# High and low activations joined in one product of 512 columns, loops written out, and the FFN's order of casts, drains and waits changed

## What is computed

```python
def swiglu_ffn(h, w_in, w_out):
    g, u = jnp.split(h @ w_in, 2, axis=-1)
    return (jax.nn.silu(g) * u) @ w_out
```

## Time and profile before

| | |
|---|---|
| median of 3 runs | 3946.58 us (3941.61 to 3947.43) |
| the profiled execution | 3947.24 us, its span 3945.5 us |
| mean granted clock of TensorE | 0.967 |
| TensorE busy | 3680.2 us, 93% |
| VectorE (DVE) busy | 2140.2 us, 54% |
| ScalarE (ACT) busy | 1617.5 us, 41% |
| moved by DMA | 612.34 MB, 155 GB/s |

### The profile page before, as it was taken

One profiled execution on the slowest core, in us unless ns is written; L12 is line 12 of the kernel. 1 busy time (PEld: TensorE's weight loads), 2 busy tenths in 40 slices (PEclk: granted clock), 3 DMA queues, 4 the chain that ended last, 5 costly groups with the idle time before them and its releaser, 6 DMA issues.

```text
span 3945.5 us, 60283 instructions
## 1 busy us (share of the span) xinstructions
PE 3680.2 (93%) x24695; PEld 3366.3 (85%) x24695; DVE 2140.2 (54%) x2737; ACT 1617.5 (41%) x2144; POOL 241.6 (6%) x232
## 2 busy tenths in 40 slices
PE   7888799999997999989999999999989899999998
PEld 6766799999977997768989989899777699899897
DVE  5887634555656545555444444554555554444444
ACT  4334323655643333444433333343333354333333
POOL 3562000000000020000000000000000000000000
PEclk9988899999998999989999999999998899999999
DMA  7324456555454564435656656555324356566564
GB/s 207 97 86 145 136 150 181 140 151 149 139 192 124 175 160 128 150 107 149 175 183 184 182 186 180 184 164 160 124 90 135 101 159 181 181 181 181 182 185 144
DMA packets 859333, 612.34 MB, mean 155 GB/s; under 512 B 10370, under 2 KB 752305, under 8 KB 858144
## 3 DMA queue, kind: packets, MB, share of 16 engines
q1 hardware_dynamic: 857072, 602.21, 52.3%
q0 software_dynamic: 2096, 7.81, 0.7%
HBM read 607.82 MB, written 2.16 MB: 155 GB/s over the span
## 4 chain that ended last, share of the span: by engine, by line
PE 83%; DVE 9%; ACT 3%; issue 2%; POOL 2%; DMA 0%; ACTq 0%; DVEq 0%; SPq 0%
PE acc L897 48%; PE acc L887 27%; PE psC L990 2%; DVE wL L1658 2%; PE psA L959 1%; ACT wH L1256 1%; DVE xtok L1619 1%; PE psC L945 1%; DVE arena L1965 1%; PE psB L945 1%; PE psB L973 1%; ACT L1256 1%; POOL arena L760 0%; PE psA L862 0%; DMA xtok<-in_x 0%
## 5 line engine op out<-in xcount | busy, mean ns | idle before, releaser
L1658 DVE TENSOR_TENSOR wL<-ring,wH 128x1024 fp32r<-128x1024 f32 x1128 | 1336.4, 1226 | 1125.3 <-ACT wH L1256 1120.6
L897 PE MATMUL acc<-actH,wH 128*128 128x256 f32 x5760 | 1654.8, 287 | 28.4 <-DVE wL L1658 28.4
L897 PE MATMUL acc<-actL,wH 128*128 128x256 f32 x5760 | 1632.4, 283 | 0.0
L897 PE MATMUL acc<-actH,wL 128*128 128x256 f32 x5760 | 1632.1, 283 | 0.0
L1256 ACT CAST wH<-ring 128x1024 fp32r<-128x1024 f32 x1128 | 1125.1, 1046 | 1223.2 <-PE acc L887 631.9
L897 PEld LDWEIGHTS acc<-actH,wH 128*128 128x128 f32 x5760 | 1108.3, 192 | 40.7 <-DVE wL L1658 23.0
L897 PEld LDWEIGHTS acc<-actL,wH 128*128 128x128 f32 x5760 | 1108.3, 192 | 4.8 <-issue 3.3
L897 PEld LDWEIGHTS acc<-actH,wL 128*128 128x128 f32 x5760 | 1107.7, 192 | 0.0
L887 PE MATMUL acc<-wH,actH 128*128 128x512 f32 x896 | 365.5, 408 | 25.9 <-DVE actL L1650 22.8
L887 PE MATMUL acc<-wL,actH 128*128 128x512 f32 x896 | 356.6, 398 | 0.0
L887 PE MATMUL acc<-wH,actL 128*128 128x512 f32 x896 | 355.7, 397 | 0.0
(11 more groups left out here) (294 smaller groups left out, 2488.1 us busy)
## 6 DMA issues: line engine op xcount, KB each, us to landing
ring<-in_w_ffn_in SPq DMA_DIRECT2D x176, 1024.0 KB, 5.7
ring<-in_w_ffn_out SPq DMA_DIRECT2D x88, 1024.0 KB, 5.1
ring<-in_b_w_in SPq DMA_DIRECT2D x64, 1024.0 KB, 6.2
ring<-in_w_in_ab SPq DMA_DIRECT2D x56, 1024.0 KB, 5.5
ring<-in_w_in_c SPq DMA_DIRECT2D x48, 1024.0 KB, 5.7
ring<-in_kv_w SPq DMA_DIRECT2D x24, 1024.0 KB, 5.6
ring<-in_a_w_in SPq DMA_DIRECT2D x16, 1024.0 KB, 7.1
ring<-in_w_xkv SPq DMA_DIRECT2D x16, 1024.0 KB, 5.7
```

The source lines that it names most:

```text
L897: ins = pe.matmul(dst, w[:, t, f * P:(f + 1) * P], x[:, t, :], start=t == 0 and n == 0, stop=t == ph.kt - 1 and n == 2)
L1658: dve.tensor_tensor(wL[:, split_slot, cols], ring[:, slot, cols], wH[:, split_slot, cols].bitcast(F32), ALU.subtract).then_inc(l_made, 1)
```

## The change

**The joined product.** actH and actL become the two halves of one tile act2. A feat phase that is `joined` computes per k-tile wH times both halves in one product of 512 columns, and then wL times the high half, added to the right half of the bank. The sum of left and right half is the outcome: ACT copies the left half out (`take_left`), DVE adds the right one (`add_right`). Joined are the phases named above; s5, kv_mem, b_z, ab_rg and glu stay as they were. A joined chunk takes a whole bank per feature tile, both banks of its pair.

**Loops written out.** `rep` is gone; `dense` and `stream` are Python loops on all engines. Waits for turned tiles and for splits now stand only in the first iteration.

**FFN.** Roundings of weights come ahead of drains, as in the diff; silu now reads SBUF, and a third tile `up_left` takes the left half of the up product. ffn_out waits for hidL block by block, in its first chunk.

```diff
-        actH = sb("actH", P, FT, T, dt=F32R)
-        actL = sb("actL", P, FT, T, dt=F32R)
+        act2 = sb("act2", P, FT, 2, T, dt=F32R)
+        actH, actL = act2[:, :, 0, :], act2[:, :, 1, :]
...
+        def take_left(act, ph, i, c, dst):
+            act.wait_ge(blocks_done, ph.blocks_before(i, c, ph.blocks))
+            first = 2 * ph.pair(c)
+            act.copy(dst, acc[:, first:first + 2, 0:T]).then_inc(left_out, 1)
+
+        def add_right(dve, ph, i, c, dst, left):
+            dve.wait_ge(left_out, ph.lefts(i, c))
+            first = 2 * ph.pair(c)
+            return dve.tensor_tensor(dst, left, acc[:, first:first + 2, T:2 * T], ALU.add)
...
@@ TensorE, one_block @@
-                    if c == 0 and splits:
+                    if i == 0 and c == 0 and splits:
                         pe.wait_ge(act_l, split_steps(splits[0]) + b + 1)
+                    if i == 0 and c == 0 and ph.hidden:
+                        pe.wait_ge(hid_l, hidden_before + ph.kt // 2 * (b + 1))
...
+                elif ph.joined:
+                    bank = pair[:, b, :]
+                    for t in range(ph.kt):
+                        if turn_call is not None and i == 0 and c == 0 and b == 0:
+                            pe.wait_ge(turned_l, FT * turn_call + t + 1)
+                        pe.matmul(bank.rearrange("p (h t) -> p h t", h=2), high[:, t, :], act2[:, t, :, :],
+                                  start=t == 0, stop=False)
+                        ins = pe.matmul(bank[:, T:2 * T], low[:, t, :], xH[:, t, :], start=False,
+                                        stop=t == ph.kt - 1)
...
@@ dense, on every engine @@
-                with rep(pe, ph.iters) as i:
+                for i in range(ph.iters):
...
@@ TensorE, FFN @@
-                    pe.wait_ge(hid_l, (l * FFN_T + sum(FFN_PARTS[:k + 1])) // 2)
-                    dense(ffn_out)
+                    dense(ffn_out, hidden_before=(l * FFN_T + sum(FFN_PARTS[:k])) // 2)
...
@@ ACT, one_block @@
-                if b == ph.blocks - 1 and fn is not None:
+                if b == ph.blocks - 1 and ph.joined:
+                    take_left(act, ph, i, c, feat_slot(ph, fn, i, c))
+                elif b == ph.blocks - 1 and fn is not None:
                     drain_chunk(act, ph, i, c, fn)
...
@@ ACT, FFN (cast = split_weights of block k of iteration i) @@
+                    for i in range(ffn_in.iters):
+                        cast(i, 1)
+                        if i > 0:
+                            take_left(act, ffn_in, i - 1, 1, up_left)
+                        cast(i, 2)
+                        if i > 0:
+                            hidden_high(i - 1)
+                        cast(i, 3)
+                        wait_past(act, drained[ffn_in.pair(1)], ffn_in.pair_uses(i, 1))
+                        take_left(act, ffn_in, i, 0, silu_g)
+                        act.wait_ge(drained[ffn_in.pair(0)], ffn_in.pair_uses(i, 0) + 1)
+                        act.activation(silu_g, silu_g, ACT.Silu).then_inc(silu_done, 1)
+                        cast(i, 4)
+                    take_left(act, ffn_in, ffn_in.iters - 1, 1, up_left)
+                    hidden_high(ffn_in.iters - 1)
...
@@ DVE, one_block @@
+                if b == ph.blocks - 1 and ph.joined:
+                    dst = feat_slot(ph, fn, i, c)
+                    add_right(dve, ph, i, c, dst, dst).then_inc(drained[ph.pair(c)], 1)
...
@@ DVE, FFN @@
+                    def up(i):
+                        add_right(dve, ffn_in, i, 1, hid_f, up_left).then_inc(up_summed, 1)
+                        dve.wait_ge(silu_done, i + (pairs_done + 1))
+                        dve.wait_ge(up_summed, i + (pairs_done + 1))
+                        dve.tensor_tensor(hid_f, hid_f, silu_g, ALU.mult).then_inc(drained[ffn_in.pair(1)], 1)
...
+                    for i in range(ffn_in.iters):
+                        low(i, 1)
+                        if i > 0:
+                            up(i - 1)
+                        low(i, 2)
+                        if i > 0:
+                            hidden_low(i - 1)
+                        low(i, 3)
+                        add_right(dve, ffn_in, i, 0, silu_g, silu_g).then_inc(drained[ffn_in.pair(0)], 1)
+                        low(i, 4)
+                    up(ffn_in.iters - 1)
+                    hidden_low(ffn_in.iters - 1)
```

More of the change, by code:

```diff
@@ L132, in __init__ @@
         plan["chunks"] += chunks
+        self.joined, self.joined0 = joined, plan["joined"]
+        plan["joined"] += chunks if joined else 0
         self.end = plan["chunks"]
@@ L347, in program @@
         out_done = sem("out_done")
-        plan = {"blocks": 0, "chunks": 0}
+        plan = {"blocks": 0, "chunks": 0, "joined": 0}
         def columns(w, kt, cols):
@@ L354, in columns, with feat @@
             return lambda j, k=0: v[:, k * kt:(k + 1) * kt, bass.ts(j, cols)]
-        def feat(w, first, tiles, iters=1):
+        def feat(w, first, tiles, iters=1, joined=True):
             at = columns(w, FT, P)
@@ L369, in tok @@
                          "tok", iters, hidden)
-        s5_u = feat(a["a_w_in"][0], 0, 8, 2)
-        s5_z = feat(a["a_w_in"][0], 8, 8, 2)
-        kv_mem = [(feat(a["w_xkv_2"][l], 0, XH), tok(a["w_xkv_2"][l], 1, 1, 4)) for l in range(DEPTH)]
+        s5_u = feat(a["a_w_in"][0], 0, 8, 2, joined=False)
+        s5_z = feat(a["a_w_in"][0], 8, 8, 2, joined=False)
+        kv_mem = [(feat(a["w_xkv_2"][l], 0, XH, joined=False), tok(a["w_xkv_2"][l], 1, 1, 4)) for l in range(DEPTH)]
         glu_at = columns(a["a_w_glu"][0], 8, 2 * P)
@@ L383, in program @@
             b_q.append(feat(a["b_w_in"][0], 8 * hh, 8, 2))
-            b_z.append([feat(a["b_w_in"][0], NH * (r + 1) + 8 * hh, 8, 2) for r in range(BRANCHES)])
+            b_z.append([feat(a["b_w_in"][0], NH * (r + 1) + 8 * hh, 8, 2, joined=False) for r in range(BRANCHES)])
         nsa_counts = [1] * 16 + [2] * 8 + [1] * 24
@@ L1462, in _ @@
                            ACT.Sigmoid).then_inc(gate_ready, 1)
-            for ph in kv[1:]:
-                dense(ph)
-            dense(b_q[0])
+            dense(kv[1])
+            dense(kv[2], kwT)
+            dense(kv[3])
+            dense(b_q[0], qT)
             def silu_z(k):
@@ L1553, in _ @@
             turn_out(TURN_MIX[1], G_MIX + 16)
-            dense(c_q)
-            blocks = join(block_steps(c_k), block_steps(c_v))
+            dense(c_q, dqT)
+            blocks = join(block_steps(c_k, dkT), block_steps(c_v))
             alternate(head_roots(norm_c), blocks, [2] * 8 + [1] * 4)
@@ L1671, in dense @@
             def dense(ph, fn=None, then=None):
-                with rep(dve, ph.iters) as i:
+                for i in range(ph.iters):
                     for c in range(ph.body):
```

105 lines of the change are left out of this document (42 added, 63 removed).

## The result

The changed kernel takes 3919.78 us (median of 5 runs, 3905.74 to 3920.65) against 3945.46 for the kernel before (3941.61 to 3947.43). The ratio is 0.9924 [0.9905, 0.9944]. That is 26 us won where 72 were forecast, and the median lies above the range of 3860 to 3903. The direction was right, the size was not. The profiled execution took 3920.65 us with a span of 3918.9. The five times lie in two groups, three from 3919.78 to 3920.65 us and two at 3905.74 and 3908.73, and the profile is one of the slower group.

What follows compares the result with a forecast made beforehand. TensorE's products were taken as the bound, each paying 13.3 ns beyond its columns. Terms -59.7 - 13.1 - 9.9 - 4 + 11.2 + 3.5 = -72.0 took 3947.2 to 3875 us, range 3860 to 3903.

Steps and rivals of the forecast that it cites:

- The joined product: In 280 joined feat blocks, a k-tile goes from 0.360 to 0.3467 us: -59.7 us, lower bound 0.
- rival C: The fixed part is per 256 columns of moving activations, so the join saves 0: 3935 us; chance 0.04.
- A: The forecast itself: 3875 us, own range 3864 to 3887; chance 0.73.
- Loops written out: First FFN part of each layer: table loads leave the loop and its 0.86 us stalls go, -13.1 us.
- From ffn_in to ffn_out: At the six ffn_in ends, block-by-block hidL waits shorten the stop: -9.9 us, and -4 us from fewer clock falls.
- Head-norm stages: Two-step drains at 16 chunk ends in kv_cmp, ab_nk and c_k: +11.2 us; five bare phase-end drains: +3.5 us.
- Rival B: The 16 head-norm pauses grow and drop the clock, 1.5 us each, at most +24: up to 3899 us; chance 0.09.
- The rest at nothing: DMA fetches, ACT and DVE branches, extra code fetch and TensorE weight loads across the kernel cost 0.
- Rival F: More is won than counted, as pauses in attention shrink with the blocks: about 3850 us; chance 0.04.

## Why the prediction missed

By its own steps:

1. **The joined product: wrong in its size.** The step that failed is "0.360 us becomes 0.2267 + 0.120 = 0.3467. [...] I take it whole". Each pitch was read where products of one width follow each other, and I added them for an order in which the widths alternate. Alternating, a k-tile costs 353.3 ns, in a few stretches 346.7 (below); the mean over the run at full clock is 351.4, so 4480 of them save 4480 x 0.0086 = 39 us and not 60, and the FFN's longer last drains take 6.3 of that back. The bound from below, 0, was kept for rival C alone, and the own range of A did not carry it (3864 to 3887; its two parts at their bounds give about 3857 to 3888, and neither holds the result): no row of before showed a wide product behind a narrow one, and that was the unknown to widen for.
2. **Loops written out: right in the stage.** 13.4 us measured alone, for 13.1, by the table loads as said. Of the whole time 4.7 us were won alone.
3. **From ffn_in to ffn_out: right in mechanism.** -16.1 for -13.9, with the stop after block 0 at 1.04 us where I had 1.2; it comes from the join. The falls of the clock went with the stop, and the run without the new wait shows that they would be worse now.
4. **Head-norm stages: right in mechanism, too cheap.** The drain was costed at 0.7 a chunk. At a chunk's end of c_k it now is, from the copy's start to the spread product, 2.17 us (2700.72 to 2702.89), before 1.56:

```profile
2700.72 0.59 ACT L527 COPY arena<-acc 128x512 f32<-128x512 f32 x1 [3.59 <-PE acc L903]
```

```profile
2701.34 0.69 DVE L533 TENSOR_TENSOR arena<-arena,acc 128x512 f32<-128x512 f32 x1 [2.77 <-ACT arena L527]
...
2702.15 0.69 DVE L1727 SCALAR_TENSOR_TENSOR probT<-ident,head_rms 128x512 f32<-128x512 f32 x1
```

```profile
2702.89 1.41 PE L961 MATMUL psC<-probT,mean_of 128*128 128x512 f32 x2 [1.42 <-DVE probT L1727]
```

That is +0.61, as costed. But the sum is short of the clock: c_k has 10.2 us at 0.50 where it had none, and lost 6.1 us where 8 x 0.7 less 3.4 for its join is 2.2. **Rival B came true**, in c_k and most of all in a place that neither it nor the sum named: the pause ahead of W1, of the same kind, costs 12.0 us, since the clock does not come back while W1 runs, and 2.2 more in kv[0] behind it. This is the second step that failed: the sum put the clock after these pauses at nothing. I gave B 0.09 on the ground that three stops of that length had brought no fall. But three of the six had brought one, which is an even chance for each longer pause; and B's price of 1.5 us a fall was read where the clock came back after 3 us, not where it stays down for 34.
5. **The rest at nothing: right for the DMAs** (0.66 share, fetches in 5.8 us). In c_v, c_out and the others the trace shows +9.3 us. 6 of these are c_v's, and the second execution of the same kernel does not have them; the written loops may have a part in them, which no run settles.

In numbers, ffn_in 14.9, the other dense phases 5.2, norm stages and W1 18.3 and the rest 9.3, less 2.2 won more at ffn_out, make the 45.5 us between 3875.2 and 3920.65. Rival C is out: in every joined stage the mean k-tile at full clock is 346.7 to 353.4 ns, and with the wide products in a row it has their 226.7. Rival F is out by the time. By the 2.5 ns of the Trainium skill (TensorE: Matmul & The Clock Gate, section Back-to-back issue gap), which the page gives for a single product by itself, the join would have saved 11.2 us, an estimate from the page; the pitches in the trace make it 39.

The version that puts the products of one width together, leaves the three norm stages as they were and casts ahead at ffn_out reached 3877.99 us. Its time is near the forecast's, but not by the forecast's sum.

## What to carry to other kernels

A pitch read from a row of equal instructions holds for that row: before two pitches are added, look for a place where the two kinds alternate, and if there is none, widen the range by it or group the instructions by kind. A second drain was free where the next block covered it and dear where TensorE waited for it: join by stage, not everywhere. A pause of TensorE that grows, here by 0.6 us, can cost the stage behind it at half clock, here 12 us: give that a price and a chance. And measure an edit over the stages behind it too: c_k took 6 us less without its join, and c_v behind it mostly as much more.

## What the hardware showed beyond the forecast

**The order of widths has a price, in a pattern that locks.** Alternating, the distances of starts mostly repeat 236, 113, 233, 117, 241, 120 ns (353.3 a k-tile). In the first ffn_in part of the second layer they repeat 233, 117, 231, 112 in the changed kernel, near 346.7 a k-tile, and the part took 188.97 us; in the second execution of the same kernel it took 192.38. Of the six profiled executions that alternate there in the changed order, three took 188.97 or 188.98 us and three 192.37 or 192.38. A part of ffn_in kept its pattern from end to end. What picks it is open.

**At half clock nothing is paid beyond the columns.** Where the clock is 0.50 in the changed kernel, the next product starts 427 ns after a wide joined one (22 of 23, within 1 ns) and 213 or 214 ns after a narrow one (all 26), that is 512 and 256 columns at 1.2 GHz. The Trainium skill (TensorE: Matmul & The Clock Gate, section Back-to-back issue gap) has the columns over 1.2 GHz there, and the trace agrees; at full clock it has 2.5 ns beyond them for a single product by itself, where these operands, in rows of equal width, show 13.3.

**TensorE at work can stay at half clock.** W1's 128 products ran 27.22 us at 0.50 with no idle time between, in one execution of a kernel, and 16.98 in another with the same pause ahead. Why it is so in six executions of seven is open, as is what makes c_v's clock fall in some.
